# A recurrent scan on one Trainium2 core: where the transpose of a triangular inverse is made, its levels in two halves, and filler products at three steps

## The reference

```
def _wkv7_step(S, inp):
    r, w, k, v, kk, a = inp
    sa = jnp.einsum('bhvk,bhk->bhv', S, kk)
    S = S * w[:, :, None, :] - sa[..., None] * (kk * a)[:, :, None, :] + v[..., None] * k[:, :, None, :]
    y = jnp.einsum('bhvk,bhk->bhv', S, r)
    return S, y
...
    _, y_fwd = lax.scan(_wkv7_step, S0, (r_t, tm(decay[0]), tm(kd[0]), v_t, kk_t, tm(a[0])))
    _, y_bwd = lax.scan(_wkv7_step, S0, (r_t, tm(decay[1]), tm(kd[1]), v_t, kk_t, tm(a[1])), reverse=True)
```

## Time and profile before

| | |
|---|---|
| median of 3 runs | 2680.83 us (2669.11 to 2684.38) |
| the profiled execution: its own time, its span | 2684.5 us, 2682.7 us |
| PE, PEld, DVE, ACT busy over the span | 96%, 89%, 75%, 58% |
| mean granted TensorE clock over the span | 0.968 of full speed |
| the scan in this execution | about 560 to 845 us of the span |

### The profile page before, as it was taken

One profiled execution on the slowest core, in us unless ns is written; L12 is line 12 of the kernel. 1 busy time (PEld: TensorE's weight loads), 2 busy tenths in 40 slices (PEclk: granted clock), 3 DMA queues, 4 the chain that ended last, 5 costly groups with the idle time before them and its releaser, 6 DMA issues.

```text
span 2682.7 us, 56874 instructions
## 1 busy us (share of the span) xinstructions
PE 2572.7 (96%) x24560; PEld 2385.4 (89%) x24560; DVE 2011.1 (75%) x3094; ACT 1557.2 (58%) x2536; POOL 51.1 (2%) x58
## 2 busy tenths in 40 slices
PE   7999999989999999999999999999998899999999
PEld 7779998868887899999999999999897799988999
DVE  4555547785444599999999999999866788575884
ACT  4434434474333477777777777777665565464662
POOL 0001100000000000000000000000003000000000
PEclk9989999978998999999999999999999999999999
DMA  6113442200001399999999999999732254441443
GB/s 245 64 71 120 183 177 95 101 1 4 20 5 65 111 348 362 346 350 358 345 361 343 369 336 369 332 377 340 286 134 94 79 189 174 174 167 55 179 175 124
DMA packets 83266, 538.59 MB, mean 201 GB/s; under 512 B 9488, under 2 KB 9616, under 8 KB 38976
## 3 DMA queue, kind: packets, MB, share of 16 engines
q1 hardware_dynamic: 82368, 530.68, 53.7%
q0 software_dynamic: 640, 4.20, 0.4%
HBM read 533.80 MB, written 1.05 MB: 199 GB/s over the span
## 4 chain that ended last, share of the span: by engine, by line
PE 86%; DVE 7%; ACT 5%; issue 1%; DMA 0%; DVEq 0%; ACTq 0%; SPq 0%; PEldq 0%
PE ps L570 23%; PE ps L571 23%; PE ps L572 23%; PE ps L1443 2%; PE ps L576 1%; DVE sl L532 1%; PE ps L1952 1%; PE ps L585 1%; PE ps L1421 1%; PE ps L1437 1%; PE ps L1428 1%; DVE xl L566 1%; PE ps L808 1%; ACT sh L525 1%; PE ps L2096 1%
## 5 line engine op out<-in xcount | busy, mean ns | idle before, releaser
L2178 DVE TENSOR_TENSOR sl<-ring,sh 128x1024 fp32r<-128x1024 f32 x613 | 718.0, 1219 | 14.0 <-ACT sh L2136 11.0
L2136 ACT ACTIVATE sh<-ring 128x1024 fp32r<-128x1024 f32 x613 | 609.2, 1061 | 3.1 <-DVE xl L2022 1.9
L570 PE MATMUL ps<-sh,xh 128*128 128x256 f32 (+2 forms) x2012 | 570.3, 283 | 10.5 <-DVE sl L532 9.5
L572 PE MATMUL ps<-sh,xl 128*128 128x256 f32 (+2 forms) x2012 | 569.8, 283 | 0.0
L571 PE MATMUL ps<-sl,xh 128*128 128x256 f32 (+2 forms) x2012 | 569.5, 283 | 0.0
L570 PE MATMUL ps<-xh,sh 128*128 128x256 f32 (+2 forms) x1856 | 536.5, 289 | 24.5 <-DVE sl L532 13.4
L571 PE MATMUL ps<-xl,sh 128*128 128x256 f32 (+2 forms) x1856 | 531.6, 286 | 0.0
L572 PE MATMUL ps<-xh,sl 128*128 128x256 f32 (+2 forms) x1856 | 528.5, 285 | 0.0
L532 DVE TENSOR_TENSOR sl<-ring,sh 128x1024 fp32r<-128x1024 f32 (+1 forms) x341 | 399.5, 1198 | 70.2 <-ACT sh L525 69.8
L525 ACT ACTIVATE sh<-ring 128x1024 fp32r<-128x1024 f32 (+1 forms) x341 | 338.8, 1021 | 114.4 <-PE ps L572 107.8
L570 PEld LDWEIGHTS ps<-sh,xh 128*128 128x128 f32 x2012 | 379.6, 189 | 21.4 <-DVE sl L532 4.7
(11 more groups left out here) (556 smaller groups left out, 4012.7 us busy)
## 6 DMA issues: line engine op xcount, KB each, us to landing
ring<-ws_d SPq DMA_DIRECT2D x229, 1024.0 KB, 7.2
ring<-ws_d SPq DMA_DIRECT2D x80, 1536.0 KB, 6.3
ring<-ws_d SPq DMA_DIRECT2D x225, 512.0 KB, 6.5
ring<-ws_d SPq DMA_DIRECT2D x24, 1408.0 KB, 6.3
ring<-ws_d SPq DMA_DIRECT2D x4, 1256.0 KB, 5.4
ring<-ws_d SPq DMA_DIRECT2D x2, 1088.0 KB, 5.0
scan_t<-scn_d POOLq DMA_DIRECT2D x1, 1828.0 KB, 7.4
ring<-ws_d SPq DMA_DIRECT2D x1, 1248.0 KB, 5.8
```

What stands on the lines that cost most here:

```text
L570: e.matmul(out, ah, bh, start=start, stop=False)
L572: return e.matmul(out, al, bh, start=False, stop=stop)
L2136: e.activation(out, raw(u)[:, a:z], ACT.Copy).then_inc(*af.on("high", u, i))
L2178: e.tensor_tensor(l, raw(u)[:, a:z], f32(h), SUB).then_inc(s_fd if i < 2 else s_fp, 1)
```

## The change

It has four parts, all in the scan.

1. Y is no longer computed by TensorE. After each masked copy into `X` (levels 0 to 4) VectorE transposes X in blocks of 32x32 into `Y`. The inverted blocks are at most 32 wide when Y is read, so these are all that is needed. The products Ut (16 a chunk) and Y (64 a chunk) go, with their copies, and so does the write of the identity to `Y` by ScalarE.
2. For that, each head's X, T and Z now lie in the half of the partitions of its own G: everything is addressed by `part(0, i)` and `slot(i, p)` where it was `own(p)` and `i`. T and X now read the half i // 4 and write the half i // 4. N reads and writes i // 4; the first part of Z reads the other half and writes i // 4; its second part reads p and writes i // 4.
3. Every level is split in two halves by p: 8 products of T, 8 of T, a copy by ScalarE for each; 8 of X, 8 of X, a masked copy and a transpose by VectorE for each. One PSUM bank serves a half.
4. `fill(b)` adds a product of 128 rows and 256 columns whose result nobody reads, ahead of Z, of N and of y/S: three in a chunk.

The core of the diff:

```diff
         def g_slot(i, p):
-            return 8 * (i // 2 % 2) + 4 * p + 2 * (i // 4) + i % 2
+            return 8 * (i // 4) + 4 * p + i % 4
...
+            def fill(b):
+                e.matmul(PS[:, b, 0:256], con("o1024"), con_t[:, WARM:WARM + 256], start=True, stop=True)
...
-                    b, free = psum.take(("Ut", *u), 2)
-                    w.wait_ge(*free)
-                    for i, p in HEADS:
-                        last = e.matmul(PS[part(0, i, cn), b + p, col(i, cn)], d.AR[own(p), 0, i, cs], d.BK[own(p), 0, i, cs], start=True, stop=True)
-                    last.then_inc(*pe.on("Ut", *u))
...
                     for lv in range(1, 6):
-                        b, free = psum.take(("T", *u, lv), 2)
-                        w.wait_ge(*free, dv["Y", *u, lv - 1])
-                        for i, p in HEADS:
-                            last = e.matmul(fours(PS[own(p, cn), b:b + 2, 0:128], lv)[:, i // 4, i % 4], d.G[part(0, i, cn), g_slot(i, p), 0:cn],
-                                            side(d.Y[part(0, i, cn), y_slot(i, p), :], lv, d.y_side), start=True, stop=True)
-                        last.then_inc(*pe.on("T", *u, lv))
+                        for p in range(2):
+                            b, free = psum.take(("T", *u, lv, p))
+                            w.wait_ge(*free, dv["Y", *u, lv - 1, p])
+                            for i in TILES:
+                                h = part(0, i, cn)
+                                last = e.matmul(halves(PS[h, b, 0:128], lv, 4)[:, i % 4], d.G[h, g_slot(i, p), 0:cn], side(d.Y[h, slot(i, p), :], lv, d.y_side), start=True, stop=True)
+                            last.then_inc(*pe.on("T", *u, lv, p))
                         yield
-                        w.wait_ge(ac["T", *u, lv], dv["X", *u, lv - 1])
-                        if lv < 5:
-                            b, free = psum.take(("Y", *u, lv), 2)
...
+                        for p in range(2):
+                            b, free = psum.take(("X", *u, lv, p))
+                            w.wait_ge(*free, ac["T", *u, lv, p], dv["X", *u, lv - 1, p])
+                            for i in TILES:
+                                h = part(0, i, cn)
+                                last = e.matmul(spread(PS[part(0, i), b:b + 1, :], lv)[:, i % 4], d.T[h, slot(i, p), :], side(d.X[h, slot(i, p), :], lv, d.x_side), start=True, stop=True)
+                            last.then_inc(*pe.on("X", *u, lv, p))
...
                     b, free = psum.take(("Z", *u), 2)
-                    w.wait_ge(*free, ac["Vt", *u])
+                    w.wait_ge(*free)
+                    fill(b)
+                    w.wait_ge(ac["Vt", *u])
                     for i, p in HEADS:
-                        last = e.matmul(PS[own(p, cn), bank(b, i), col(i)], d.G[part(1, i, cn), g_slot(i, p), 0:cn], ...
+                        last = e.matmul(PS[part(0, i, cn), b + p, col(i)], d.G[part(1, i, cn), g_slot(i, p), 0:cn], ...
...
-                        last = e.matmul(PS[part(0, i), b + p, col(i)], d.X[own(p, cn), i, :], d.Z[own(p, cn), i, :], start=True, stop=True)
+                        last = e.matmul(PS[part(0, i), b + p, col(i)], d.X[part(0, i, cn), slot(i, p), :], d.Z[part(0, i, cn), slot(i, p), :], start=True, stop=True)
...
+                    for p in range(2):
+                        e.transpose(runs_of(d.Y, p), runs_of(d.X, p)).then_inc(*dv.on("Y", *u, 0, p))
                     yield
                     for lv in range(1, 6):
                         yield
...
+                        for p in range(2):
+                            b, x = psum["X", *u, lv, p], d.X[:, 4 * p:4 * p + 4, :]
+                            w.wait_ge(pe["X", *u, lv, p])
+                            e.copy_predicated(side(x, lv, d.x_side), level_mask(d.x_level, lv, d.x_side, 4), spread(PS[:, b:b + 1, :], lv)).then_inc(*dv.on("X", *u, lv, p))
+                            psum.gone["X", *u, lv, p] = [dv.now()]
+                            if lv < 5:
+                                w.wait_ge(dv.now())
+                                e.transpose(runs_of(d.Y, p), runs_of(d.X, p)).then_inc(*dv.on("Y", *u, lv, p))
```

More of the change, by code:

```diff
@@ L1318, in side, with halves @@
             return v.rearrange("q i (b s m) -> q i b s m", s=2, m=m)[:, :, :, s, :]
-        def halves(v, lv):
-            return v.rearrange("q (i b m) -> q i b m", i=8, m=2 ** lv)
+        def halves(v, lv, n):
+            return v.rearrange("q (i b m) -> q i b m", i=n, m=2 ** lv)
         def spread(v, lv):
@@ L1360, in streams, with runs_of @@
                 runs = [g for g in runs if next(g, "end") != "end"]
+        def runs_of(v, p):
+            return v[:, 4 * p:4 * p + 4, :].rearrange("q i t -> q (i t)")
         def y_first(n, c):
@@ L1431, in steps @@
-                        yield
-                        w.wait_ge(ac["T", *u, lv], dv["X", *u, lv - 1])
-                        if lv < 5:
-                            b, free = psum.take(("Y", *u, lv), 2)
[L1435 to L1444, removed]
+                        for p in range(2):
[5 more added lines that the diff above has]
+                            last.then_inc(*pe.on("T", *u, lv, p))
@@ L1445, in steps @@
                         yield
                     b, free = psum.take(("Z", *u), 2)
-                    w.wait_ge(*free, ac["Vt", *u])
+                    w.wait_ge(*free)
+                    fill(b)
+                    w.wait_ge(ac["Vt", *u])
                     for i, p in HEADS:
-                        last = e.matmul(PS[own(p, cn), bank(b, i), col(i)], d.G[part(1, i, cn), g_slot(i, p), 0:cn], d.NV[part(1, i, cn), 2 * i + p, :], start=i % 4 == 0, stop=not ci and i % 4 == 3)
+                        last = e.matmul(PS[part(0, i, cn), b + p, col(i)], d.G[part(1, i, cn), g_slot(i, p), 0:cn], d.NV[part(1, i, cn), 2 * i + p, :], start=i % 4 == 0, stop=not ci and i % 4 == 3)
@@ L1456, in steps @@
                                 w.wait_ge(across)
-                            last = e.matmul(PS[own(p, cn), bank(b, i), col(i)], d.AR[own(p), 0, i, cs], d.S[own(p), i, :], start=False, stop=i % 4 == 3)
+                            last = e.matmul(PS[part(0, i, cn), b + p, col(i)], d.AR[own(p), 0, i, cs], d.S[own(p), i, :], start=False, stop=i % 4 == 3)
                     last.then_inc(*pe.on("Z", *u))
@@ L1460, in steps @@
                     b, free = psum.take(("N", *u), 2)
-                    w.wait_ge(*free, ac["Z", *u], dv["X", *u, 5])
+                    w.wait_ge(*free)
+                    fill(b)
+                    w.wait_ge(ac["Z", *u], dv["X", *u, 5, 0], dv["X", *u, 5, 1])
                     for i, p in HEADS:
-                        last = e.matmul(PS[part(0, i), b + p, col(i)], d.X[own(p, cn), i, :], d.Z[own(p, cn), i, :], start=True, stop=True)
+                        last = e.matmul(PS[part(0, i), b + p, col(i)], d.X[part(0, i, cn), slot(i, p), :], d.Z[part(0, i, cn), slot(i, p), :], start=True, stop=True)
                     last.then_inc(*pe.on("N", *u))
@@ L1470, in steps @@
                     w.wait_ge(*free)
+                    fill(by)
                     if ci:
@@ L1548, in identity @@
                         w.wait_ge(*([pe["N", n, ci - 1]] if ci else [dv["prepared", n, 1]]))
-                        for v in (d.X, d.Y):
-                            e.activation(v, sn("id2")[:, None, :].broadcast_to([128, 8, 64]), ACT.Copy).then_inc(*ac.on())
-                        ac.mark("identity", n, ci)
+                        e.activation(d.X, sn("id2")[:, None, :].broadcast_to([128, 8, 64]), ACT.Copy).then_inc(*ac.on("identity", n, ci))
                 identity(0)
@@ L1570, in steps @@
                     for lv in range(1, 6):
[L1571 to L1574, removed]
+                        for p in range(2):
+                            w.wait_ge(pe["T", *u, lv, p])
+                            e.activation(side(d.T[:, 4 * p:4 * p + 4, :], lv, d.y_side), halves(PS[:, psum["T", *u, lv, p], 0:128], lv, 4), ACT.Copy).then_inc(*ac.on("T", *u, lv, p))
+                            psum.gone["T", *u, lv, p] = [ac.now()]
                         yield
@@ L1674, in steps @@
                         yield
[L1675 to L1681, removed]
-                    for x in range(2):
[L1683 to L1686, removed]
+                    w.wait_ge(ac["identity", *u], dv.now())
+                    m = sn(f"{d.x_level}0")[:, d.x_side:C:2].bitcast(u32)[:, None, :].broadcast_to([128, 8, C // 2])
+                    for x in range(2):
+                        e.copy_predicated(d.X[own(x), :, d.x_side:C:2], m[own(x)], d.G[own(x), 8 * x:8 * x + 8, d.x_side:C:2]).then_inc(*dv.on())
+                    for p in range(2):
+                        dv.mark("X", *u, 0, p)
+                    w.wait_ge(dv.now())
+                    for p in range(2):
+                        e.transpose(runs_of(d.Y, p), runs_of(d.X, p)).then_inc(*dv.on("Y", *u, 0, p))
                     yield
```

10 lines of the change are left out of this document (4 added, 6 removed).

## The result

The changed kernel takes 2703.53 us (median of 20 runs, 2691.01 to 2719.77) where the kernel before takes 2680.77 us (20 runs, 2667.18 to 2708.33). The ratio is 1.0077, with a 95% interval of 1.0056 to 1.0099: slower by 23 us. The forecast was 2704 us and +23 us. The number was met; the three terms that it was summed from (work, waits, clock) were each off, and the errors cancelled.

A forecast was written before the change was run, and what follows sets the result against it. TensorE's queue bounds the scan (PE busy 228.4 of 245 us). Terms 28 - 2 - 4 + 5 - 4 = +23 us on 2684.5 give 2707.5, or 2704 as a median; range 2670 to 2722 us.

The forecast's parts named there:

- work: TensorE's queue in the scan: products dropped, slower T, Z and N, and fillers sum to +2.5 us a chunk, +25 us.
- waits: PE's waits in the scan: fillers in idle time, ScalarE's copies of T and VectorE's transposes, -2, -4 and +5 us.
- clock: Half-clock windows in the scan: fillers end them a little earlier, -4 us; added work partly at half clock makes 25 into 28.
- -2, -4 and +5: PE's waits: 2 us back for fillers in idle time, 4 us gained at ScalarE's copies, 5 us lost to late transposes.
- Two products in a row for one quarter: In Z and N, if the queue cannot pass the second product, some +0.9 us a chunk, kept for the upper end.
- rival D: Quarters of the array don't count; T, Z and N keep their pace: -34 us, 2670 us; chance 0.06.
- ScalarE's copies of T: Copying T in halves while PE makes the second half removes most of PE's 4.6 us wait: -4 us.
- the transposes: VectorE's ten a chunk at 0.45 us each deliver late where both directions are at X, then T: +5 us.
- Rival A: Three fillers a chunk hold the clock at 2.4 GHz through the stretch: 2684 us, no change; chance 0.20.
- B: PE stands at least 0.63 us before each Z, N and y, so fillers cost nothing: 2663 us, clock held; chance 0.12.
- C: PE waits for VectorE's transposes at 0.64 us (+7), sparse levels keep half clock longer (+17): 2728 us; chance 0.12.

The follow-up runs named there:

- e1: The changed kernel without its 30 fillers ahead of Z, N and y; ratio 0.9989 to the kernel before.
- g2: The changed kernel with its fillers replaced by 15 ahead of direction 0's T, from the third chunk on; 2665.05 us median, ratio 0.9940 to the kernel before.
- e2: The kernel before plus the same 30 fillers at Z, N and y, nothing else changed; ratio 1.0017 to the kernel before.
- e3: The kernel before with only the order of T's 16 products changed; ratio 0.9995 to the kernel before.
- f4: The kernel before plus 24 fillers ahead of T from the third chunk on; ratio 0.9984 to the kernel before.
- f3: The changed kernel, its fillers replaced by 24 ahead of T from the third chunk on and ten ahead of direction 1's first G; ratio 0.9987 to before.

## Why the prediction came out right

By luck, as far as the number goes. The forecast of +23 us is 25 of work, -1 of waits (-2, -4 and +5) and -1 of clock (+3 for the part of the work that runs at half clock, and -4). The profile has +18.8, -9.7 and +14.5. The errors are -6, -9 and +15 us, and they cancel.

The work was read rightly, though a third too high in sum. Y and Ut gave 24.7 us (24.6 forecast), the fillers took 18.2 (19), N 4.7 (4.4), Z's first part 3.8 (4.5), and T 17.7 (21.5, ten chunks at +2.15; two levels lie ahead of 600 us, and T's start-to-start time before was 0.50 on average, not 0.43, which was one row). X rose by 1.4, and the steps that the change leaves alone fell by 2 together. Two products in a row for one quarter cost Z nothing and N a little. T at 0.84 us refutes rival D. The rule of "TensorE: Matmul & The Clock Gate", Part 3, in the Trainium skill, by which a weight load overlaps running products only when the row group differs, does not hold for these products: T alternates between two row groups before and after, and takes twice as long. The transpose took 0.446 us for my 0.45; the estimate of 0.62 from the Trainium skill's page "VectorE: DVE Perf Modes" (The three transpose paths) was too long.

The waits were wrong. For ScalarE's copies of T I forecast -4, and PE's waits for them went from 6.0 us to 1.0. For the transposes I forecast +5, and they cost at most 2, because copy and transpose overlap and come to 0.66 to 0.81 us a pair: a late half of T waited 0.2 us at most (0.5 behind level 0) where I had 0.4 twice. Beyond that, 6.5 us of "issue" stops went. I had named 2.4 of them as part of PE's waits and not counted any as something that the change could move.

The clock was wrong in sign. I gave it -4 with the reason that dense products stand where the low windows end. e1 shows no such return in the changed kernel, and the low time of the changed kernel's scan grew by 29 us in the profiled run (+14.5 us) and by 16 to 25 us in the mean of all runs (+8 to +12). What I had named only as a counterweight, that T keeps two quarters busy instead of four, fits this, but no run changes the number of quarters alone.

Rival A was near the truth in the old layout only, B was refuted by e1 (the fillers cost 20 us), C had the right sign and nearly the size for the clock (+17) but not for VectorE.

## What to carry to other kernels

Count a step of small products by the quarters of the array that it keeps busy, not by the products: dropping 80 of some 380 products a chunk paid for nothing more than putting the others in two quarters instead of four. A filler is paid in full wherever PE is the bound, so it pays only where it wins the clock back, and that has to be measured over many runs: in the changed layout 15 ahead of T gave 0.5% (e1 to g2) and 30 ahead of Z, N and y cost 0.9% (e1 to the changed kernel). Whether the ones ahead of T work as dense products or by filling the stops there is not separated. When runs of one kernel scatter, split each run's time by its mean clock; the rest scatters by 1 to 4 us where the clock's part does by 4 to 13, and shows effects of a few us.

## What the runs showed of the hardware that I had not expected

The "issue" stops of PE, 3.6 to 6.7 us in the scan, stand in every kernel with the dense old levels (before, e2, e3, f4) and in none with the new layout. The traces say what ends them. On queue 8 instructions are read in pieces of 16 KB: 58 pieces in the scan before, 47 after (600 us to the last product of y):

```profile
q8 instruction: 58, 0.95, 1.7%
...
q8 instruction: 47, 0.77, 1.2%
```

The scan has 14784 products and weight loads in PE's records before and 11895 after, so a piece is worth some 255 of PE's records in both. In the four profiles with such stops, all 35 that are longer than 0.15 us end 1.2 to 1.6 us after such a read has ended. The reads are some 4 us apart, so by chance this would hold for about one in ten. No run varied the supply alone, but this leaves little room for another cause: the stops are PE waiting for its own instructions. T in four quarters uses up 64 records in 0.43 us; at that pace a piece would last 1.7 us (an estimate from these rows), well under the 4 us between reads. Fewer products and slower ones both ease this; how much each did was not measured apart.

A full PE does not keep the clock: it stayed at 1.2 GHz through 53 us in which PE was busy 52.68 (e1), though all 16 gate products of the bonus stream (272 columns each, eight of them with 128 rows) stand among the steps there. In g2 it was at 2.4 GHz through 198 us, with one 128-row filler ahead of each T of direction 0 from 692 to 800 us; but f3, with those fillers and nine more ahead of T, has 27 us at 1.2 GHz in the same place (807.7 to 835), so one profile of either kind proves no rule.
